# Two attention units per step in the second block of a four-layer kernel

## The reference

```python
for layer in range(DEPTH):                       # DEPTH = 2
    ada = einsum('bd,de->be', silu(c), w_ada[layer]) + b_ada[layer]
    shift, scale, gate = split(ada, 3)
    h = rms_norm(x, norm_g[layer]) * (1 + scale) + shift
    y = even_mixer(h, ...) if layer % 2 == 0 else odd_mixer(h, ...)
    x = x + gate * y
return rms_norm(x, final_g)
```

## Time and profile before

| | |
|---|---|
| median of 3 runs | 1550.85 us (1548.6 to 1552.39) |
| span of the profiled execution | 1547.1 us |
| PE busy in it | 1524.0 us (99%) |
| DVE busy | 1026.7 us (66%) |
| ACT busy | 440.3 us (28%) |
| DMA queues' packets, share of 16 engines | 44.8% (largest queue) |
| chain that ended last, by engine | PE 93%, DVE 4%, issue 1%, ACT 1% |

### The profile page before, as it was taken

One profiled execution on the slowest core, in us unless ns is written; L12 is line 12 of the kernel. 1 busy time (PEld: TensorE's weight loads), 2 busy tenths in 40 slices (PEclk: granted clock), 3 DMA queues, 4 the chain that ended last, 5 costly groups with the idle time before them and its releaser, 6 DMA issues.

```text
span 1547.1 us, 27734 instructions
## 1 busy us (share of the span) xinstructions
PE 1524.0 (99%) x11151; PEld 1351.3 (87%) x11151; DVE 1026.7 (66%) x1928; ACT 440.3 (28%) x932; POOL 12.5 (1%) x26
## 2 busy tenths in 40 slices
PE   8999999999999999999999999999999999999998
PEld 7988869898899999898878899799999787678887
DVE  5788886577667774578897467667765564535562
ACT  5434424012100001334423201300011456524441
POOL 1000000000000000100000000000000000000000
PEclk9999999999999999999999999999999999999999
DMA  8443453353475454343343442475454745463320
GB/s 285 175 164 110 150 152 110 110 203 123 147 235 164 159 174 162 134 166 119 114 149 99 164 140 93 150 272 164 158 178 157 261 146 216 178 227 120 133 107 28
DMA packets 172385, 243.40 MB, mean 157 GB/s; under 512 B 16830, under 2 KB 95332, under 8 KB 172260
## 3 DMA queue, kind: packets, MB, share of 16 engines
q1 hardware_dynamic: 170372, 237.96, 44.8%
q10 hardware_dynamic: 1888, 3.67, 0.6%
HBM read 240.56 MB, written 1.05 MB: 156 GB/s over the span
## 4 chain that ended last, share of the span: by engine, by line
PE 93%; DVE 4%; issue 1%; ACT 1%; DMA 0%; SPq 0%; DVEq 0%; POOL 0%; ACTq 0%
PE psum L629 34%; PE psum L1644 27%; PE psum L1499 6%; PE psum L3105 3%; PE psum L1299 2%; PE psum L445 2%; PE psum L1558 2%; PE psum L3197 2%; PE psum L428 2%; PE psum L1428 1%; PE psum L461 1%; PE psum L3205 1%; PE psum L663 1%; PE psum L1400 1%; PE psum L1294 1%; PE psum L1553 1%
## 5 line engine op out<-in xcount | busy, mean ns | idle before, releaser
L629 PE MATMUL psum<-hT,ring 128*128 128x256 f32 x1552 | 342.8, 380 | 0.2 <-ACT hT L3302 0.2
L629 PEld LDWEIGHTS psum<-hT,ring 128*128 128x128 f32 x1552 | 292.3, 190 | 44.6 <-issue 6.0
L629 PE MATMUL psum<-uT,ring 128*128 128x256 f32 x384 | 84.9, 380 | 0.0
L1644 PE MATMUL psum<-hT,ring 128*128 128x128 f32 x704 | 82.4, 275 | 1.0 <-issue 1.0
L629 PEld LDWEIGHTS psum<-uT,ring 128*128 128x128 f32 x384 | 72.6, 190 | 10.4 <-DVE uT L1162 0.6
L1644 PEld LDWEIGHTS psum<-hT,ring 128*128 128x128 f32 x704 | 80.4, 192 | 1.5 <-issue 1.5
L1925 ACT ACTIVATE SCR<-SCR 128x512 f32<-128x512 f32 x22 | 13.9, 630 | 219.9 <-DVEq L2706 219.9
L510 DVE TENSOR_TENSOR psum<-psum,const 128x512 f32<-128x512 f32 (+4 forms) x41 | 22.1, 559 | 65.1 <-PE psum L445 64.1
L491 ACT ACTIVATE SCR<-psum,stats 128x128 f32<-128x128 f32 (+2 forms) x128 | 49.9, 407 | 22.5 <-DVE stats L524 22.4
L1644 PE MATMUL psum<-G,ring 128*128 128x128 f32 x400 | 47.8, 276 | 0.0
L1920 ACT ACTIVATE SCR<-psum 128x256 f32<-128x256 f32 (+1 forms) x30 | 10.7, 356 | 127.9 <-PE psum L1644 127.9
(11 more groups left out here) (647 smaller groups left out, 3046.5 us busy)
## 6 DMA issues: line engine op xcount, KB each, us to landing
ring<-in_w_in SPq DMA_DIRECT2D x46, 1024.0 KB, 7.0
ring<-in_ffn_w_gate_up SPq DMA_DIRECT2D x88, 512.0 KB, 5.6
ring<-in_w_ada SPq DMA_DIRECT2D x24, 1024.0 KB, 8.0
ring<-in_ffn_w_down SPq DMA_DIRECT2D x16, 1024.0 KB, 6.1
ring<-in_w_in_odd SPq DMA_DIRECT2D x16, 1024.0 KB, 7.4
ring<-in_w_in_even SPq DMA_DIRECT2D x10, 1024.0 KB, 7.1
ring<-in_x_w_kv SPq DMA_DIRECT2D x8, 1024.0 KB, 5.9
ring<-in_ssm_w_glu SPq DMA_DIRECT2D x8, 1024.0 KB, 5.9
```

Of the source, the lines that this page charges most:

```text
L629: ins = nc.tensor.matmul(b[0:width, n * S:n * S + S], w[k // 4][:, k % 4, c0[n]:c0[n] + width], tile(k), start=k == 0, stop=k == kt - 1)
L1644: ins = nc.tensor.matmul(banks[job][:, at:at + P], left, right, start=first, stop=last)
```

## The change

A step is now a visit of two units. In visit v PE turns both units of visit v-1, does the outputs of both units of visit v-2, the scores of both of visit v, then the fill of that visit. `scores` is called with both units and takes all four banks (and both rotary waits) before its first product. ACT copies the two turned units, then does both exponentials, then the fill's copies. DVE stores v-2, does both maxima, then both rows. In visit 0, `windows(1)` stands between maxima and rows. There are 10 visits in the even layer and 6 in the odd one. There are three places for turned rows instead of two, and two row slots instead of three; the copy of a pair's second unit waits until the place has been read. The fill tables are rewritten. Three of four `even out` products are split 6 + 1 + 1 tiles over visit 7, visit 8 and the end (before: 6 + 2). c0, c4 and c5 are no longer stored raw and gated later, but like the other c units. One piece of weights (`ada11`) is loaded ahead of `za`.

```diff
-    def pe(self, nc, pe, i):
-        if 0 <= i - PAIR_LAG - 1 < len(self.u):
-            self.outputs(nc, pe, i - PAIR_LAG - 1)
-        if i < len(self.u):
-            self.scores(nc, pe, (i,))
-        if 0 <= i - PAIR_LAG < len(self.u):
-            self.turn(nc, pe, i - PAIR_LAG)
+    def pe(self, nc, pe, v):
+        for i in visit(v - 1, len(self.u)):
+            self.turn(nc, pe, i)
+        for i in visit(v - 2, len(self.u)):
+            self.outputs(nc, pe, i)
+        scored = visit(v, len(self.u))
+        if scored:
+            self.scores(nc, pe, scored)
...
+    def act(self, nc, act, v):
+        turned, scored = visit(v - 1, len(self.u)), visit(v, len(self.u))
+        for i in turned:
+            if i >= len(self.turned) and i != turned[0]:
+                self.column_read(act, i - len(self.turned), scored)
+            self.copies(nc, act, i)
+        for i in scored:
             self.exponentials(nc, act, i)
...
+    def dve(self, nc, dve, link, v, between=None):
+        for i in visit(v - 2, len(self.u)):
+            self.stored(nc, dve, i)
+        for i in visit(v, len(self.u)):
             self.maxima(nc, dve, link, i)
...
+        if between:
+            between()
+        for i in visit(v, len(self.u)):
+            self.rows_normed(nc, dve, link, i)
...
+def visit(v, of):
+    return [i for i in (2 * v, 2 * v + 1) if 0 <= i < of]
...
-AB_FILL = {0: ["kvc"], 1: ["ks"], 2: ["vs", "qb0"], 3: ["qb1", "hidden v", "hidden k"],
...
+AB_FILL = [["kvc", "ks", "vs"],
+           ["qb0", "hidden v", "hidden k"],
+           ["hidden v turned", "hidden k turned", "qb1", "k cmp", "v cmp"],
+           ["zb0", "zb1"],
+           ["zb2", "zb3", "silu b", "ada11"],
+           ["part ada11", "za0", "za1", "ada12"],
+           ["part ada12", "za2", "za3", "silu a", "ada13"],
+           ["part 0", "part 1", "part 2"],
+           ["more 0", "more 1", "more 2"],
+           ["part ada13"]]
+C_FILL = [["q1", "k1", "Z0 a", "Z0 b"],
+          ["q2", "k2", "Z0 c", "Z0 d", "silu c"],
+          ["q3", "k3", "V1 a", "V1 b"],
+          ["V1 c", "V1 d", "Z1 a", "Z1 b", "Z1 c", "Z1 d", "silu d"],
+          ["part 0", "part 1", "part 2"],
+          []]
-RAW = {0: 0, 4: 4, 5: 5}
...
-            if i == 1:
-                windows(1)
-            if i == 2:
+            att_ab.dve(nc, dve, link, v, (lambda: windows(1)) if v == 0 else None)
+            if v == 0:
                 rope("kvc", raw[:, 0:2, :])
                 windows(0)
```

More of the change, by code:

```diff
@@ L379, in __init__ @@
         self.negmax_ready, self.rows_ready = sems
-        self.probs, self.turned = scratch
+        self.probs, self.row_slots, self.turned = scratch
         self.stats, self.ident, self.base = stats, ident, base
-        self.steps = len(units) + PAIR_LAG + 1
+        self.visits = range(-(-len(units) // 2) + 2)
     def stat(self, i, kind):
@@ L566, in pair_masks, with visit_jobs @@
              const("causal").unsqueeze(1).unsqueeze(1).broadcast_to([P, 2, 2, P]))]
-def pair_jobs(units, fill=None):
+def visit(v, of):
+    return [i for i in (2 * v, 2 * v + 1) if 0 <= i < of]
+def visit_jobs(units, fill):
     names = []
-    for i in range(len(units) + PAIR_LAG + 1):
-        if i < len(units):
+    for v, filling in enumerate(fill):
+        for i in visit(v - 1, len(units)):
+            names += [f"{units[i]} turned {s}" for s in range(1 if units[i].endswith("cmp") else 2)]
+        for i in visit(v, len(units)):
             names += [f"{units[i]} scores {n}" for n in range(2)]
[L574 to L577, removed]
+        names += [x for x in filling if not x.startswith(("silu", "part", "more"))]
     return names
@@ L2838, in second_pieces @@
     wide("zb", w, E_ZB, 512, "zb3")
+    ada(1, 1)
     wide("za", w, E_ZA, 512, "za3")
-    for n in (1, 2, 3):
-        ada(1, n)
+    ada(1, 2)
+    ada(1, 3)
     for n in range(2):
@@ L3130, in ab_fill @@
                     out_part("even", n, range(6), even_tile)
+                elif name.startswith("more"):
+                    out_part("even", n, range(6, 7), even_tile)
                 elif name == "kvc":
@@ L3148, in ab_fill @@
                     transposed(name, wide(name[:-1]), (P * n,), hT, KT, (P,))
-        for i in range(att_ab.steps):
-            att_ab.pe(nc, pe, i)
-            ab_fill(i)
+        for v in att_ab.visits:
+            att_ab.pe(nc, pe, v)
+            ab_fill(v)
         def finish(prefix, first, tile_done):
@@ L3217, in _ @@
             odd_job(name)
-        for i in range(att_c.steps):
-            att_c.pe(nc, pe, i)
-            for name in C_FILL.get(i, []):
+        for v in att_c.visits:
+            att_c.pe(nc, pe, v)
+            for name in C_FILL[v]:
                 if name.startswith("part"):
@@ L3347, in ab_fill @@
         def ab_fill(i):
-            for name in AB_FILL.get(i, []):
+            for name in AB_FILL[i]:
                 n = int(name[-1]) if name[-1].isdigit() else None
-                if name.startswith("part"):
+                if name.startswith(("part", "more")):
                     continue
@@ L3379, in ab_fill @@
                     copy(name, z[:, n + (4 if name[1] == "b" else 0), :], 0, S)
-        for i in range(att_ab.steps):
-            att_ab.act(nc, act, i)
-            ab_fill(i)
+        for v in att_ab.visits:
+            att_ab.act(nc, act, v)
+            ab_fill(v)
         square(2)
@@ L3407, in _ @@
             odd_copy(name)
-        for i in range(att_c.steps):
-            att_c.act(nc, act, i)
-            for name in C_FILL.get(i, []):
+        for v in att_c.visits:
+            att_c.act(nc, act, v)
+            for name in C_FILL[v]:
                 if name.startswith("silu"):
```

96 lines of the change are left out of this document (39 added, 57 removed), and 4 rows, old and new, of the table AB_FILL.

## The result

The changed kernel takes 1562.04 us (median of 5 runs, 1559.58 to 1564.31), the kernel before 1548.60 in the runs beside them (1546.79 to 1552.39): ratio 1.0078, interval 1.0063 to 1.0092. By the ratio that is 12 us slower (10 to 14; the two medians lie 13.4 apart); the forecast was 7.7 slower, 1558.5, in a range of 1550 to 1566. The profiled execution of the changed kernel is the fastest of its five: 1559.58, with a span of 1557.8.

A forecast was written before the change was run, and what follows sets the result against it. PE was taken to set the pace (busy 111.39 of 113.00 us in the even attention). From 1550.85: -6.0 grouping - 2.3 present waits - 2.6 old fall + 14.3 new waits + 4.3 new falls = +7.7, 1558.5 us; range 1550 to 1566.

The forecast's parts named there:

- The waits: New PE waits at five places plus shorter ones, as two units' softmax must fit in one fill: +14.3 us (10 to 18).
- `even out0`: Its first part takes the bank of b3 win's second head directly behind that pair's scores: PE waits 4.9 us.
- c4's scores: Scores of c4 and c5 need all four banks, one awaiting c2's copy behind silu c: wait 2.9 us (2 to 4.3).
- The grouping: PE changes product kind half as often: 0.50 us saved per pair, 12 pairs in both layers, -6.0 us (-1.2 to -9.2).
- The falls: Two new falls of PE's clock likely behind new idle times, 2.15 us each: +4.3 us (0 to 10.4).
- The fall of the kernel before: Clock fall after the short waits at 1336 to 1342, late in the even attention, would go: -2.6 us.
- - 2.3: PE's present waits would go: 1.61 us in the even attention and 0.72 before c4's scores.
- No new fall: Rival: the same forecast without the 4.3 us of new clock falls, 1554.2 us; chance 0.15.
- Falls at every cluster: Rival: four clock falls at 2.6 us, 10.4 instead of 4.3, giving 1564.6 us; chance 0.10.
- Grouping pays more: Rival: pair scores at the first block's pace, 0.77 us saved per pair, 9.2 in all, no fall: 1551.0; chance 0.12.
- Early waits don't come: Rival: DVE and ACT run 1 to 2 us ahead near the start, 5.8 us of waits go: 1552.7; chance 0.04.
- A drain behind each load: Rival: each ACT table load adds a drain, making the even out0 wait 1.4 us longer: 1559.9 us; chance 0.02.

The follow-up runs named there:

- run 3: The changed kernel with DVE's windows(1) behind the rows of a0 and a1 instead of ahead of them: 1556.66 us, ratio 1.0042 to the kernel before.
- run 6: The changed kernel with three odd-layer moves: silu c between copies and exponentials, V1's first two mixes behind visit 1's rows, third behind Z0 d: 1557.76 us, 1.0045.
- run 7: The changed kernel with the moves of run 3, run 5 and run 6 together: 1551.07 us, ratio 1.0005 to the kernel before.
- run 1: The changed kernel with a small Exp behind silu a on ACT, bringing the exponentials' table back early: 1562.35 us, ratio 1.0079 to the kernel before.
- run 5: The changed kernel with ada12 and ada13 moved into visit 7 ahead of even out0's first part, and the small Exp behind silu a: 1560.42 us, 1.0064.
- run 9: The kernel before in its even layer, with the odd layer in visits and the three moves of run 6: 1548.30 us, ratio 0.9990 to the kernel before.
- run 2: The changed kernel with V1's first two weight mixes on DVE moved from behind Z0 b to behind visit 1's rotary step: 1563.94 us, 1.0090.
- run 4: The changed kernel, product kinds alternating: first unit by unit, banks reordered (1590.56 us, 1.0263); second only turning and outputs alternating, banks kept (1561.57 us, 1.0078).
- Run 8: The kernel of run 7 with the small Exp on ACT behind the copies of visit 7 instead of behind silu a: 1548.14 us, 0.9990.

## Why the prediction was right, point by point

**The waits: right, +14.3 against 13.9.** Place by place: the first turnings 2.1, measured 1.8 (1.3 and 0.5, for DVE's rows); ahead of b0's scores 1.9, measured 1.5 (0.2 and 0.8 at the turning of a3, 0.5 at the scores); `qb1` 1.1 and the turning behind it 0.7, measured 1.1 and 0.6; `even out0` 4.9, measured 4.8; c4's scores 2.9, measured 3.4. The wait at a3's turning is the one for `qb0`'s copies:

```profile
1275.74 0.44 PE L462 MATMUL psum<-const,SCR 128*128 128x128 f32 x2 [0.77 <-ACT uT L3289]
```

The wait at c4's scores was right for the wrong start, so that its size is in part luck: I had let PE's arrival and DVE's softmax set it; in the trace V1's weights land at 1448.7 and DVE's first mix follows at once, ahead of the maxima of c2 and c3 and all that follows from them:

```profile
1435.98 12.69 DMA ring<-in_w_in_odd
...
1448.77 1.24 DVE hg L3616
```

Run 3, where they landed 1.1 earlier against the start of the odd attention, has 2.5. Run 6 shows that the end of the chain is as the prediction put it, Z0 c, Z0 d, silu, copies. Runs 3 and 6, one place each, and run 7, three together, show that these waits, with the falls behind them, are the loss. Runs 1 and 5 don't show it for `even out0`: most of what they took from that wait came back at the scores of `b3 win`.

**The grouping: its size was off.** The step that failed is the saving of 0.50 for each of 12 pairs, 6.0 us. To see it, the clock has to be taken out. The even layer of the changed kernel and that of run 6 are the same instructions; 3.57 us of work ran at 1.2 GHz in the one and 7.47 in the other, and PE's busy time differs by 1.90: 0.49 for each such us. With half of this work taken off, the even stretch has 132.6 before the change (135.62, with 6.1 at half clock; run 9, with the same even layer, gives 132.6 too) and 131.9 after (133.69): 0.7 saved for 8 pairs, 0.1 each. The odd one has 119.6 and 117.6: 2.0 for 4 pairs, 0.5 each as forecast (0.49 by run 6). In all -2.7 in place of -6.0.

What the even layer lacks can be told in part. From each PE instruction's start to the next one's, without idle time and with the same correction, the attention products of a pair went from 4.75 to 4.41 us in the odd layer and only from 4.39 to 4.26 in the even one, where four of the eight pairs have a cmp unit with fewer records and I had counted them like the others. Fill and output products got 0.7 shorter in the odd layer and 0.3 longer in the even one; I had counted the output products as unchanged, while their parts now change kind once more in visit 8. Waits seem to cost busy time too: corrected in the same way, the even stretch has 131.4 in run 3 and 130.8 in run 7, where waits are gone (run 7 also has another order of fill). Which of these makes the difference between the layers stays open.

**The falls: two were forecast, two are in the profile, and more executions seem to have three.** The windows of the changed kernel around its two long waits and behind the first ones:

```profile
1280.00:1290.00 10.00, 8.87 (x49) 7.83 (x49) 5.30 (x15) 5.82 (x21) 0.00 (x0) 1.00 0.00 0
1346.00:1356.00 10.00, 5.18 (x24) 4.24 (x21) 5.01 (x20) 4.89 (x19) 0.00 (x0) 0.66 1.05 406
1466.00:1476.00 10.00, 6.57 (x42) 5.06 (x37) 7.24 (x12) 5.33 (x13) 0.00 (x0) 0.83 0.40 141
```

1346 to 1356 has a mean clock of 0.66 and 1466 to 1476 of 0.83; 1280 to 1290 is undisturbed. Runs 1, 2, 5, 6 and the second one of 4 have nearly the same first waits and a fall there, as the row for 1282 to 1292 in run 6 shows. The other four executions of the changed kernel have no trace here; their mean clock over the whole is 0.992 or 0.993, against 0.994 in the profiled one, which is some 3 to 6 us more at 1.2 GHz. Run 8 has a fall there although the first turnings don't wait for rows any more, so these waits alone don't decide it. The even stretch of run 6 is 1.94 longer than that of the changed kernel for that fall and for the one behind `even out0`, which came later against the wait, though its idle time, 10.19, is the same. The price, 4.3, was near: 1.8 + 1.7 in the profiled execution (half of 3.57 and 3.41 us of work at 1.2 GHz; by the stretches 119.27 less 117.71, 1.6, for the second), 1.9 more in such others. The fall of the kernel before cost 3.0 (half of 6.1) and not 2.6, since fill behind the output product ran slowly too.

**The sum.** In the profiled pair: -2.7 (grouping) - 2.3 - 3.0 + 13.9 + 3.5 = +9.4, against 6.61 + 2.68 = 9.3 measured. The terms are read from the same two stretches, so that they add up is a check of the reading and no more. With 1.9 more of clock it is 11.2, which is in the interval of 10 to 14 that the times give. Against that, the forecast of 7.7 was low by grouping (3.3) and falls (1.1) and high by the waits and the old fall (0.4 each).

**The rivals.** No new fall: out, as the profile has two. Falls at every cluster: in part, two or three at 1.7 to 1.9 and not four at 2.6. Grouping pays more: out, 0.1 and 0.5 a pair, and 0.15 to 0.22 for two changes (run 4). Early waits don't come: out, 5.8 were forecast and 5.0 came. A drain behind each load: out, by run 1, where the wait fell by the load's 1.3, and by the trace, where the exponentials begin 0.02 after the load (1348.18 + 1.28, next at 1349.48).

## What to carry to other kernels

When one engine is busy 99% of the time, grouping its work saves a few tenths of a microsecond per group, but it also puts two units' chains on the other engines between one visit and the next; follow each chain against the work that covers it, and look above all at what stands ahead in the same queue only because of the order in which it is written (a window step, a silu, a table load). Three places mended took back what the change had cost. A wait that one move takes away can come back at the next place on the same queue: the early table took 1.3 us from one wait and gave 1.2 to another. Look too at which buffer the next job takes: the same products in another order cost 28 us here, some 19 of them as idle time of PE, nearly all in waits for banks, and most of the rest in the clock.

## What the runs showed of the hardware

A wait of PE costs more than its length when the clock falls behind it, and the same waits do this in one execution and not in the next: a mean clock of 1.00 in the changed kernel's 1280 to 1290, and 0.83 in run 6 at the same place with the same waits ahead (to 0.1 us). What it costs is half of the work that runs at 1.2 GHz: 1.90 us for 3.90 more of such work in the same even layer, so a fall that lies on idle time costs less. Falls show up in the first block too, which is the same in all of these kernels: the row for 698 to 707 in the earlier trace rows has one, and the same place in the changed kernel has none:

```profile
698.00:707.00 9.00, 6.80 (x90) 6.57 (x91) 8.08 (x14) 4.14 (x6) 0.00 (x0) 1.00 0.45 161
```

But that execution has a fall at another place in the first block, where the kernel before has none:

```profile
10.00:25.00 15.00, 12.55 (x68) 10.92 (x67) 8.26 (x26) 6.85 (x12) 2.66 (x6) 0.89 0.89 313
```

The four traces with one fall in the first block (the two kernels, runs 3 and 9) begin the even attention between 1240.60 and 1241.89, the other eight, with two falls, between 1242.02 and 1244.02. A single profiled execution is therefore uncertain by 2 to 4 us here, and stretches with the same clock are what can be compared to a tenth.
